# Two decoder blocks and an S5/GLA pair on one core: order of the halves' sums, the last feed-forward step, the S5 table products and two early loads

## The reference, cut to what matters

```python
for l in range(DEPTH):                       # DEPTH = 2
    h = h + 0.5 * swiglu(rmsnorm(h, ffn1_norm[l]), ffn1_w_gate[l], ffn1_w_up[l], ffn1_w_down[l])
    ...                                      # MLA, differential and pooling branches, gated and merged
    h = h + 0.5 * swiglu(rmsnorm(h, ffn2_norm[l]), ffn2_w_gate[l], ffn2_w_up[l], ffn2_w_down[l])
x = rmsnorm(h, final_norm)
# swiglu(x, g, u, d) = (silu(x @ g) * (x @ u)) @ d      with D_FF = 2816
...
# s5_mixer, parameters only:
lam_bar = exp(lam * dt)
b_bar = ((lam_bar - 1) / lam)[..., None] * (b_re + 1j * b_im)
y = real(c @ state) + d * u                  # state[t] = lam_bar * state[t-1] + b_bar @ u[t]
```

## Time and profile before

| | |
|---|---|
| Runs, us | 1564.64, 1567.38, 1567.41 |
| Profiled execution, us | 1564.1, its span 1562.3 |
| TensorE matmul busy | 1528.3 us, 98% of the span |
| VectorE busy | 1190.9 us, 76% |
| ScalarE busy | 800.2 us, 51% |
| GpSimd busy | 44.5 us, 3% |
| HBM read | 257.83 MB, 166 GB/s over the span |
| Mean granted TensorE clock | 0.995 of full speed |

### The profile page before, as it was taken

One profiled execution on the slowest core, in us unless ns is written; L12 is line 12 of the kernel. 1 busy time (PEld: TensorE's weight loads), 2 busy tenths in 40 slices (PEclk: granted clock), 3 DMA queues, 4 the chain that ended last, 5 costly groups with the idle time before them and its releaser, 6 DMA issues.

```text
span 1562.3 us, 26661 instructions
## 1 busy us (share of the span) xinstructions
PE 1528.3 (98%) x11410; PEld 1433.2 (92%) x11410; DVE 1190.9 (76%) x1579; ACT 800.2 (51%) x1030; POOL 44.5 (3%) x43
## 2 busy tenths in 40 slices
PE   6999999999999999999999999999998999999999
PEld 5999999999999999899999999999987999999988
DVE  6786688787887776977778778878788799756844
ACT  5444356565454444544455455454554555775654
POOL 0000001210000000000001110000000000000000
PEclk9999999999999999999999999999999999999999
DMA  7455444343555554555534433447444444315531
GB/s 264 173 196 187 172 154 178 135 136 135 182 184 192 189 190 160 194 193 187 189 138 172 160 135 137 160 162 260 176 161 166 159 166 159 136 64 193 189 135 55
DMA packets 38693, 260.59 MB, mean 167 GB/s; under 512 B 4656, under 2 KB 5040, under 8 KB 9136
## 3 DMA queue, kind: packets, MB, share of 16 engines
q1 hardware_dynamic: 37856, 257.84, 46.2%
q10 hardware_dynamic: 720, 1.05, 0.2%
HBM read 257.83 MB, written 1.05 MB: 166 GB/s over the span
## 4 chain that ended last, share of the span: by engine, by line
PE 81%; DVE 11%; ACT 4%; issue 3%; DMA 1%; ACTq 0%; DVEq 0%
PE ps L203 17%; PE ps L205 16%; PE ps L204 16%; PE ps L254 16%; PE ps L256 8%; DVE w_low L193 4%; ACT w_high L186 3%; DMA w_raw<-in_weights 1%; DVE ffn_gate L234 1%; PE ps L1257 1%; DVE ffn_up L234 1%; DVE x L290 1%; PE ps L1269 1%; PE ps L2058 1%; ACT x L279 1%
## 5 line engine op out<-in xcount | busy, mean ns | idle before, releaser
L186 ACT ACTIVATE w_high<-w_raw 128x2048 fp32r<-128x2048 f32 (+3 forms) x244 | 457.7, 1880 | 398.3 <-PE ps L205 198.5
L193 DVE TENSOR_TENSOR w_low<-w_raw,w_high 128x2048 fp32r<-128x2048 f32 (+3 forms) x244 | 552.1, 2264 | 129.5 <-ACT w_high L186 126.2
L254 PE MATMUL ps<-x,w_high 128*128 128x512 f32 x1408 | 501.2, 398 | 19.0 <-DVE w_low L702 9.5
L256 PE MATMUL ps<-x,w_low 128*128 128x256 f32 x1408 | 397.3, 282 | 0.0
L254 PEld LDWEIGHTS ps<-x,w_high 128*128 128x128 f32 x1408 | 267.2, 190 | 80.1 <-issue 11.7
L256 PEld LDWEIGHTS ps<-x,w_low 128*128 128x128 f32 x1408 | 269.5, 191 | 0.1
L203 PE MATMUL ps<-x,w_high 128*128 128x256 f32 (+1 forms) x904 | 261.8, 290 | 4.5 <-DVE x L290 4.5
L205 PE MATMUL ps<-x,w_low 128*128 128x256 f32 (+1 forms) x904 | 255.7, 283 | 0.0
L204 PE MATMUL ps<-x,w_high 128*128 128x256 f32 (+1 forms) x904 | 255.6, 283 | 0.0
L203 PE MATMUL ps<-ffn_hid_high,w_high 128*128 128x256 f32 x704 | 197.4, 280 | 0.0
L204 PE MATMUL ps<-ffn_hid_low,w_high 128*128 128x256 f32 x704 | 197.2, 280 | 0.0
(11 more groups left out here) (439 smaller groups left out, 2346.5 us busy)
## 6 DMA issues: line engine op xcount, KB each, us to landing
w_raw<-in_weights SPq DMA_DIRECT2D x229, 1024.0 KB, 4.8
w_raw<-in_weights SPq DMA_DIRECT2D x10, 768.0 KB, 4.2
w_raw<-in_weights SPq DMA_DIRECT2D x5, 512.0 KB, 4.2
even_second_vectors<-in_second SPq DMA_DIRECT2D x1, 1836.0 KB, 10.4
w_raw<-in_weights SPq DMA_DIRECT2D x2, 640.0 KB, 3.9
resid<-in_x SPq DMA_DIRECT2D x4, 256.0 KB, 5.9
w_raw<-in_weights ACTq DMA_DIRECT2D x4, 256.0 KB, 7.1
out<-resid SPq DMA_DIRECT2D x3, 256.0 KB, 2.5
```

The source lines that it names most:

```text
L186: act.activation(self.wh[:, j, 0:SIZES[n]], self.raw[:, j, 0:SIZES[n]], ACT.Copy).then_inc(self.hi_made, 1)
L193: dve.tensor_tensor(self.wl[:, j, 0:SIZES[n]], self.raw[:, j, 0:SIZES[n]], self.wh[:, j, 0:SIZES[n]].bitcast(F32), ALU.subtract).then_inc( ...
L254: pe.matmul(c.bank(bank + i).rearrange("p (a t) -> p a t", a=2), wh[:, k, f], c.x[:, :, k, :], start=(k == 0), stop=False, skip_group_chec ...
L256: mm = pe.matmul(c.bank(bank + i, SEQ), wl[:, k, f], c.xh[:, k, :], start=False, stop=(k == DT - 1), skip_group_check=True)
```

## The change

Four edits:

1. `Ffn.vector`, step 0: the halves of gate(0) are added (and `gate_read` is given) ahead of the low split of slot 3, in all four feed-forward parts.
2. `Ffn.scalar`, step 10: the high splits of slots 32 and 33 stand where they stand in the other steps, ahead of silu and ahead of `high`. `Ffn.vector` is unchanged there.
3. The three S5 products go from VectorE (steps 6, 7, 8 of FFN 4) to GpSimd, which waits for the end of `coefficient` (new semaphore `values`). The `fraction` chunks move from steps 4 to 7 to steps 6 to 9. VectorE waits for the last product at the head of the even layer.
4. `Setup.sync` asks for slots 3 and 4 ahead of the vectors, positions and table; `Setup`'s work moves from steps 1 to 4 to steps 3 to 6.

```diff
@@ Ffn.scalar
         for s in range(FF_STEPS):
-            if s < LAST:
-                c.split_high(act, base + gate_at(s) + RING)
+            c.split_high(act, base + gate_at(s) + RING)
             if s == 0:
                 self.norm.root(act)
                 act.preload_act_table(ACT.Silu)
                 c.split_high(act, base + up_at(s) + RING)
             silu(s)
-            if s == LAST:
-                c.split_high(act, base + gate_at(s) + RING)
             self.aside.scalar_midway(act, s)
-            if 0 < s < LAST:
+            if s:
                 c.split_high(act, base + up_at(s) + RING)
             high(s)
             if s == LAST:
                 act.preload_act_table(ACT.Sqrt)
-                c.split_high(act, base + up_at(s) + RING)
             elif s:
@@ Ffn.vector
             take_wide(c, dve, b.gate[:, :, :], B_GATE).then_inc(b.gate_read, 1)
             if s == 0:
+                c.split_low(dve, base + gate_at(s) + RING)
                 self.norm.reciprocal(dve)
...
-            if s == 0:
-                c.split_low(dve, base + gate_at(s) + RING)
-                gate(s)
-            else:
-                gate(s)
+            gate(s)
+            if s:
                 c.split_low(dve, base + gate_at(s) + RING)
@@ Setup.sync                      (EARLY_SLOTS = 5)
         sp.wait_ge(*self.arrived(PIECES - 1))
-        c.load(sp, 2)
+        for n in range(2, EARLY_SLOTS):
+            c.load(sp, n)
         sp.dma_start(c.vec[:, DT:], self.vectors[:, DT:]).then_inc(c.vec_in, 16)
@@ Setup.vector, Setup.scalar: steps 1, 2, 3, 4 become 3, 4, 5, 6
@@ Parameters.coefficient
-        mul(self.ci, self.t1, self.m)
+        eng.tensor_tensor(self.ci, self.t1, self.m, ALU.mult).then_inc(self.values_made, 1)
@@ Tables
-        self.steps = (4, 5, 6, 7)
+        self.steps = (6, 7, 8, 9)
...
-        if s == 6:
-            e.par.outputs(dve, ln)
-        if s == 7:
-            e.par.inputs_ahead(dve, ln)
-        if s == 8:
-            e.par.outputs_ahead(dve, ln)
+    def gpsimd(self, pool):
+        par, ln = self.e.par, self.c.pool_link
+        pool.wait_ge(par.values_made, 1)
+        par.outputs(pool, ln)
+        par.inputs_ahead(pool, ln)
+        par.outputs_ahead(pool, ln)
@@ Even.vector
         self.norm.reciprocal(dve)
+        dve.wait_ge(e.par.c_made, 2)
@@ model_kernel
-                for n in range(RING, N_SLOTS):
+                for n in range(EARLY_SLOTS, N_SLOTS):
...
                 for l in range(DEPTH):
                     stages[3 * l + 1].gpsimd(pool)
+                tables.gpsimd(pool)
```

More of the change, by code:

```diff
@@ L26 @@
 PIECES = 4
+EARLY_SLOTS = 5
 FC = 2 * P
@@ L712, in vector @@
         c, ln, ang, turns = self.c, self.c.dve_link, self.ang[:, :], self.turns[:, :]
-        if s == 1:
+        if s == 3:
             dve.wait_ge(c.vec_in, 16)
@@ L718, in vector @@
             ln(dve.tensor_scalar(ang, self.pos_f[:, :], c.tab[:, T_INVF:T_INVF + 1], None, ALU.mult))
-        if s == 2:
+        if s == 4:
             reduce_angle(dve, ln, ang, turns)
             dve.tensor_scalar(turns, ang, 0.5, None, ALU.mult).then_inc(self.angle_made, 1)
-        if s == 3:
+        if s == 5:
             d, n = c.dist[:, :], self.dist_n[:, :]
@@ L728, in vector @@
             ln(dve.tensor_tensor(d, d, c.tab[:, T_CAUSAL:T_CAUSAL + 3 * P], ALU.subtract))
-        if s == 4:
+        if s == 6:
             dve.wait_ge(self.sines_made, 2)
@@ L1408, in __init__ @@
         self.t1, self.t2, self.rate, self.lr = self.dt, self.x, self.ex, self.p
-        self.dt_made, self.x_made, self.exp_made, self.th_made, self.sin_made, self.c_made, self.b_made = sems
+        self.dt_made, self.x_made, self.exp_made, self.th_made, self.sin_made, self.values_made, self.c_made, self.b_made = sems
     def rates(self, act):
@@ L1578, in __init__ @@
         self.par = Parameters(self, self.vec, small, self.cc, self.turned,
-                              [c.sem(f"par_{x}") for x in ("dt", "x", "exp", "th", "sin", "c", "b")])
+                              [c.sem(f"par_{x}") for x in ("dt", "x", "exp", "th", "sin", "values", "c", "b")])
 class Tables(Nothing):
```

## The result

| | before | after |
|---|---|---|
| Runs, us | 1564.64, 1567.38, 1567.41, 1567.91 | 1550.41, 1550.83, 1551.06, 1552.82 |
| Median, us | 1567.39 | 1550.94 |
| Profiled execution, us (span) | 1564.1 (1562.3) | 1550.83 (1549.0) |

The ratio is 0.9901, 95% interval 0.9884 to 0.9918: 16.5 us faster, against a forecast of 1551.5.

What follows compares the result with a forecast made beforehand. TensorE, busy 98% of the span, bounds the kernel, so its waits were counted: 16.9 us gained less 2.9 lost gives 14.0, 1550.1 from the profiled execution or 1553.4 from the median; forecast 1551.5, range 1538 to 1558.

Steps and rivals of the forecast that it cites:

- Term A: Start: gate(1) begins without its wait, the half clock goes, up(1) is on time; 8.5 us gained, 3.3 to 8.7.
- Term B: FFN 3: one split leaves the front of the sum of gate(0), removing that wait; 2.0 us gained, 1.5 to 2.5.
- Term C: Last feed-forward step: earlier splits and residual sums remove 1.6 us at each of four hand-overs; 6.4 us, at least 3.
- Term D: FFN 4: GpSimd's products delay VectorE, so waits before up(7) and L1689 and the half clock stay; 2.9 us lost.
- b: FFN 4: delay one GpSimd row gives a VectorE row reading SBUF twice; taken as 0.9 us, between 0.2 and 1.17.
- paid turns: FFN 4: GpSimd rows that delay VectorE, 7.6 in step 6 and 5 in step 7 up to the sum of up(7).
- time in hand: FFN 4: without GpSimd's delay, VectorE's sum of up(7) would end 2.8 us ahead of TensorE's need.
- my formula: FFN 4: the delay of L1689 is 12.6 b - 2.8, put at 8.5 us in place of 5.6.
- the rule: Skill's exclusive port lock between VectorE and GpSimd: whichever starts first keeps it; b 1.17, loss 6.3 us, time 1553.5.
- (1): FFN 4: GpSimd works in the gaps and costs VectorE next to nothing; 8.6 us gained there, time 1540; chance 0.34.
- (2): FFN 4: stretched-operand product rows each hold VectorE over 2 us, making the kernel slower, 1571.6 to 1575; chance 0.04.
- (3): Start: the wait returns at up(1) through a late slot 3 or sum; gain only 3.3, time 1556.7; chance 0.09.

Runs made afterwards that it cites:

- e3: Kernel before with edit 2 alone (both high splits of the last step at their usual places), run twice: 1556.34 us, ratio 0.9929; 1557.46 us, ratio 0.9945.
- e5: Changed kernel with the three S5 products' arithmetic replaced by MEMSETs on GpSimd: 1536.13 us, ratio 0.9825 to the kernel before.
- e6: Changed kernel with the four fraction chunks later and thinner (steps 7 to 9), products still on GpSimd: 1541.30 us, ratio 0.9860 to the kernel before.
- e7: Changed kernel with the products back on VectorE (steps 6, 7, 8), fractions as changed, GpSimd idle here: 1544.02 us, ratio 0.9878 to the kernel before.

## Why the prediction was right

**Term A, 8.5 us:** 8.4 by position at the first down slot. Order and clock were as worked out, and slot 3 was in at 19.6 us, between the 18.4 of the usual landing and the 21.6 allowed for; edits 1 and 4 alone show that both were needed. (The 52 matmuls in 6.00 us of the earlier trace rows are counted with those at the edges; 0.117 us each is the right distance from one to the next, 6.00 / 52 isn't.)

**Term B, 2.0 us:** 2.0 by position, in the profile after and in that of edit 1 alone. Another 0.4 just ahead of it in the profile after comes from edit 2 (e3 shows the same place).

**Term C, 6.4 us:** 6.3 at the hand-overs. The first matmul behind FFN 1 starts at 196.94 without a wait. Missed were the 0.4 us just named and the even layer's norm, 0.95 us: VectorE's order moves up by 2.5 us there, TensorE's by 1.6 at the hand-over and by the rest at the sum that L313 waits for. By itself edit 2 is worth 8.2 us by position, since it also takes 0.6 us of the wait in FFN 3 that edit 1 takes whole.

**Term D, -2.9 us:** -1.4 by position, -1.4 (0 to -3) by the run of edit 3 alone. The mechanism was the one forecast, its size too large: b is 0.83 us on average and not 0.9, and the paid turns are 12 and not 12.6 (12 rows up to the sum of up(7), stretched by 0.31 to 1.10 us, 10.0 together). The time in hand was too large too: step 6 starts at 1140.09, which is 1152.25 in the profile before and not 1151.65, so it is 2.2 us and not 2.8. The delay is then 10.0 - 2.2 = 7.8 by my formula. By position TensorE gets past the sum of up(7) 7.5 us late, not 8.5: 3.7 us around up(7) (2.5 of wait, the rest at the lower clock) and 3.7 of wait before L1686. The wait before up(7) was forecast at 2, that before L1689 at 6. The lower clock behind L1686 cost 0.5 us less than before. The figure 1.17 of the rule came from a row on the mixer's arena; GpSimd's first rows here take 1.05.

**Rivals.** (1) is refuted: VectorE's rows are stretched, and edit 3 alone gains nothing. (2) GpSimd's rows do last up to 3.1 us in the profile after, but those of 2.9 and more stand behind a split of VectorE's; a row with a stretched operand that meets none takes 1.05. (3) up(1) waited for nothing; in edit 1 alone, with the tables ahead of slot 3, it did.

The sum, 1550.1 to 1553.4, holds both the profiled 1550.8 and the median 1550.9. That it came out so close is partly luck, by balance: 0.95 us at the norm, 0.4 in FFN 3, 1.5 in term D and 0.4 in small places came on top, and 3.8 us by position went to a slower pace of FFN 2 and 3 in that execution (last section).

## What to carry to other kernels

A row of VectorE that meets one of GpSimd's here is late by 0.83 us on average, where a whole row of its own takes 0.69. Counted over all three products off-loading saves VectorE 1.5 us of 13.0, and it brings the cost forward, to where GpSimd happens to run; it is free only where VectorE reads PSUM, or stands idle. Ask what an off-loaded row costs the first engine, and ahead of which wait. Look first for the idle time inside VectorE's own steps, where it waits for another engine's answer, and cut the extra work so that it fits there. Two edits that act on one wait are worth it once; run each alone before adding them up.

## What the runs showed of the hardware

**Two paces at one clock.** At a granted clock of 1.00 without a wait, a pair of a 512-column and a 256-column matmul takes 347 or 353 ns, the same for hundreds of pairs. First and 32nd such pair of a gate and an up slot, in FFN 1 and FFN 2 of the profile after:

```profile
107.52 0.39 PE L255 MATMUL ps<-x,w_high 128*128 128x512 f32 x1
...
118.27 0.39 PE L255 MATMUL ps<-x,w_high 128*128 128x512 f32 x1
...
508.15 0.39 PE L255 MATMUL ps<-x,w_high 128*128 128x512 f32 x1
...
519.09 0.40 PE L255 MATMUL ps<-x,w_high 128*128 128x512 f32 x1
```

31 pairs take 10.75 and 10.94 us: 0.2 us a step, some 2 us a feed-forward part. In the second profile of the same kernel FFN 2, 3 and most of FFN 4 ran at 347; edit 2 alone differed in FFN 3 and 4 between its two profiles; the kernel before had 347, 347, 347, 353 both times. So it doesn't belong to the program alone. Both kernels whose two profiles differ were profiled on two chips, and all four profiles of one chip (the changed kernel's second, e5, e6, e7) ran FFN 1 to 4 at 347 but for single slots, so the chip may have a part in it; on the others both paces occur. What sets it isn't known; it changed at places where TensorE had stopped or changed from one kind of slot to another. The two profiles of the changed kernel differ by 4.9 us in their spans, more than most of the terms here, and the pace is the largest part of it. So positions have to be compared over stretches of one pace.

**The clock behind a wait.** Waits of 2.5 and 3.0 us before up(7) were followed by a stretch near the lower level (0.55 over 3.5 us in the profile after), the wait of 1.80 in one profile of the kernel before but not in the other; the waits of 3.08 (edit 1 alone), 2.81 (edit 4 alone) and 2.18 (e6) were followed by 1.00. With edit 3 alone the same wait before up(7) as in the profile after, 2.46 us, was followed by 1.00:

```profile
1170.50:1174.00 3.50, 3.44 (x20) 3.05 (x21) 2.39 (x2) 2.09 (x2) 3.34 (x3) 1.00 0.72 232
```

The length of the wait alone doesn't tell.
